# Transposes of a head moved to the score banks, with new step slots and a later rotation in layer 1

## What is computed

```python
def mixer_diff(h, w_in, lq1, lk1, lq2, lk2, sub_g, w_out, pos, ctx_k, ctx_v):
    z = h @ w_in                                   # 2048 x 8192
    q, k, v, g = jnp.split(z, idx, axis=-1)        # 16 heads, q and k 2 x 64, v 128
    qr = rope_2d(q, row, col)                      # latent tokens only
    k_all = jnp.concatenate([rope_2d(k, row, col), ctx_k], axis=1)
    v_all = jnp.concatenate([v, ctx_v], axis=1)
    s = jnp.einsum('bqhmd,bshmd->bhmqs', qb, k).astype(F32) * scale
    p = jax.nn.softmax(s, axis=-1)
    w = (p[:, :, 0] - lam * p[:, :, 1]).astype(v.dtype)
    o = jnp.einsum('bhqs,bshe->bqhe', w, v)
    o = rms_norm(o, sub_g) * (1 - LAMBDA_INIT_1)
    out = (o.reshape(b_, t, C_V_WIDTH) * jax.nn.silu(g)) @ w_out
```

## Time and profile before

| | |
|---|---|
| runs | 2828.07, 2830.34, 2833.81 us |
| median | 2830.34 us |
| profiled execution, device time | 2835.45 us |
| its span, first to last instruction | 2833.9 us |
| mean granted TensorE clock | 0.963 of full speed |
| TensorE matmul busy | 2570.7 us, 91% |
| VectorE, ScalarE, GpSimd busy | 1722.7, 810.6, 426.5 us |
| HBM traffic | 140 GB/s over the span |

### The profile page before, as it was taken

How to read it: one execution, slowest core, us unless ns; L and a number is a source line. 1 busy time by engine, 2 the same in 40 slices (tenths; PEclk the granted TensorE clock), 3 DMA queues, 4 the chain that set the end, 5 groups by cost and what they waited for, 6 DMA issues and landing times.

```text
span 2833.9 us, 38154 instructions
## 1 busy us (share of the span) xinstructions
PE 2570.7 (91%) x12040; PEld 2020.2 (71%) x12040; DVE 1722.7 (61%) x3165; ACT 810.6 (29%) x1698; POOL 426.5 (15%) x481
## 2 busy tenths in 40 slices
PE   6999999998888889979999999998999999978995
PEld 1258877777776768867877777777777777856884
DVE  1335777877777546766456555665666565554676
ACT  2112222222222222223233333333333333322221
POOL 0000222211222010000121212222221211011001
PEclk8999999999999989989999999999999999988998
DMA  7745544444443455554422222322232322245555
GB/s 268 251 141 174 184 138 147 128 146 150 161 161 116 144 211 182 193 189 138 136 93 86 90 72 85 95 91 85 73 97 84 97 86 93 84 135 205 182 193 200
DMA packets 165601, 395.42 MB, mean 140 GB/s; under 512 B 15008, under 2 KB 15648, under 8 KB 160992
## 3 DMA queue, kind: packets, MB, share of 16 engines
q1 hardware_dynamic: 132304, 249.08, 27.9%
q0 software_dynamic: 33168, 144.72, 14.5%
HBM read 332.93 MB, written 63.18 MB: 140 GB/s over the span
## 4 chain that ended last, share of the span: by engine, by line
PE 64%; DVE 17%; DVEq 7%; issue 5%; ACT 3%; DMA 3%; POOL 0%; ACTq 0%; SPq 0%; POOLq 0%
PE ps L554 49%; DVE w_lo L1128 4%; PE ps L440 3%; PE ps L449 3%; PE ps L583 3%; PE ps L458 3%; DVE small L1005 2%; DVE work L1022 2%; DVEq L1151 2%; DMA w_raw<-in_w_ada_dram 1%; ACT w_hi L773 1%; PE ps L541 1%; DMA stage<-z 1%; DMA o<-work 1%; DVEq L1237 1%
## 5 line engine op out<-in xcount | busy, mean ns | idle before, releaser
L554 PE MATMUL ps<-w_hi,hT_hi 128*128 128x512 f32 x2800 | 1149.6, 411 | 14.3 <-issue 7.6
L554 PE MATMUL ps<-w_hi,hT_lo 128*128 128x512 f32 x2800 | 1111.1, 397 | 0.0
L554 PE MATMUL ps<-w_lo,hT_hi 128*128 128x512 f32 x2800 | 1106.6, 395 | 0.0
L1128 DVE TENSOR_TENSOR w_lo<-w_raw,w_hi 128x512 fp32r<-128x512 f32 x560 | 408.0, 729 | 372.4 <-ACT w_hi L773 354.1
L554 PEld LDWEIGHTS ps<-w_hi,hT_lo 128*128 128x128 f32 x2800 | 534.1, 191 | 120.0
L554 PEld LDWEIGHTS ps<-w_hi,hT_hi 128*128 128x128 f32 x2800 | 536.1, 191 | 110.6 <-issue 12.3
L554 PEld LDWEIGHTS ps<-w_lo,hT_hi 128*128 128x128 f32 x2800 | 536.4, 192 | 92.6 <-issue 1.4
L773 ACT CAST w_hi<-w_raw 128x512 fp32r<-128x512 f32 x560 | 346.9, 621 | 486.3 <-PE ps L554 467.8
L1158 DVE SCALAR_TENSOR_TENSOR ada_sum<-w_raw,cond,ada_sum 128x512 f32<-128x512 f32 x480 | 365.8, 803 | 35.4 <-issue 10.3
L724 ACT ACTIVATE work<-ps,small 128x640 f32<-128x640 f32 (+1 forms) x200 | 142.1, 710 | 574.4 <-DVE small L1008 574.3
L440 PE MATMUL ps<-consts,work 128*128 128x128 f32 x768 | 133.7, 288 | 74.5 <-DVE q_low_lo L997 19.7
(11 more groups left out here) (185 smaller groups left out, 2426.9 us busy)
## 6 DMA issues: line engine op xcount, KB each, us to landing
w_raw<-in_w_in_dram SPq DMA_DIRECT2D x216, 512.0 KB, 4.0
w_raw<-in_w_ada_dram SPq DMA_DIRECT2D x256, 256.0 KB, 3.0
z<-stage POOLq DMA_DIRECT2D x27, 1280.0 KB, 5.1
w_raw<-in_w_ada_dram SPq DMA_DIRECT2D x64, 512.0 KB, 4.7
w_raw<-in_w_out_dram SPq DMA_DIRECT2D x64, 512.0 KB, 4.1
work<-z POOLq DMA_DIRECT2D x72, 320.0 KB, 3.7
work<-o POOLq DMA_DIRECT2D x8, 1280.0 KB, 8.1
x<-stage POOLq DMA_DIRECT2D x7, 1280.0 KB, 11.7
```

What stands on the lines that cost most here:

```text
L554: last = nc.tensor.matmul(ps[:, t, :], x[:, kt, t * P:(t + 1) * P], w[:, kt % RING, :], start=(kt == 0 and i == 0), stop=(kt == KT - 1 and ...
L1128: nc.vector.tensor_tensor(w_lo[:, kt % RING, :], w_raw[:, w_at(c, kt), kt % 2, :], w_hi[:, kt % RING, :].bitcast(F32), ALU.subtract).then_ ...
```

## The change

1. turn_bank: T1 (k) goes to bank 6 and T2 (mixed) to bank 7, the score banks; every other T stays in bank 5. T1 and T2 no longer wait for bank 5 but for the last exponential of the head before. In both layers. In layer 0 the wait for mod_free stands at T2 in place of S0. S0 still waits until T0, T1 and T2 have been read (t_free, four counts).
2. ORDER1: S9 stands ahead of T6 (it was behind it), so S8 and S9 follow each other.
3. AT1: new slots. T1 2 to 1, T2 4 to 2, S1 10 to 11, S2 14 to 15, S3 18 to 19, T3 24 to 26, S4 26 to 27, S7 40 to 39, S8 44 to 43, S9 48 to 45, T6 45 to 47, P1 52 to 53, B1 54 to 55; the others stand. S2 goes from row 2 to row 3, T3 from row 4 to row 5, S7 from row 8 to row 7.
4. head1: GpSimd loads q, k and v of the next head, stores the head before, then waits for P0 of the current head (pv_ready) and only then rotates.

```diff
-ORDER1 = ["T", "T", "T", "S", "S", "S", "S", "T", "S", "T", "S", "T", "S", "P", "S", "B", "S", "T", "S",
+ORDER1 = ["T", "T", "T", "S", "S", "S", "S", "T", "S", "T", "S", "T", "S", "P", "S", "B", "S", "S", "T",
           "T", "T", "P", "B", "T", "P", "B"]
...
-AT1 = [0, 2, 4, 7, 10, 14, 18, 24, 26, 28, 31, 32, 35, 36, 40, 41, 44, 45, 48, 49, 51, 52, 54, 56, 58, 59]
+AT1 = [0, 1, 2, 7, 11, 15, 19, 26, 27, 28, 31, 32, 35, 36, 39, 41, 43, 45, 47, 49, 51, 53, 55, 56, 58, 59]
...
+        def turn_bank(r):
+
+            return {1: SC, 2: SC + 1}.get(r, TURN)
...
-                bank_free(q)
+                bank = turn_bank(q)
+                if bank == TURN:
+                    bank_free(q)
+                else:
+                    pe.wait_ge(s.s_exp, h * NS + 1)
+                if bank == MOD_ROWS[0] and L.n == 0:
+                    pe.wait_ge(mod_free, 9 if isinstance(h, int) and h == 7 else h + 3)
                 for n, src in enumerate(blocks):
-                    last = nc.tensor.transpose(ps[:, TURN, n * P:(n + 1) * P], src, ident)
+                    last = nc.tensor.transpose(ps[:, bank, n * P:(n + 1) * P], src, ident)
...
                         pe.wait_ge(s.t_free, h * NF + 4)
-                        if L.n == 0:
-                            pe.wait_ge(mod_free, 9 if isinstance(h, int) and h == 7 else h + 3)
...
-                    last = nc.scalar.copy(dst[r0:r1, :], ps[r0:r1, TURN, c0:c1])
+                    last = nc.scalar.copy(dst[r0:r1, :], ps[r0:r1, turn_bank(r), c0:c1])
...
                 next_qk(L1, h + 1)
-                rotate_head(L1, h + 1)
                 if v:
                     next_v(L1, h + 1)
                 if not first:
                     store_head(L1, h - 1)
                     free_head(L1, h - 1)
+                wait(S[1].pv_ready, h * 3 + 1)
+                rotate_head(L1, h + 1)
```

More of the change, by code:

```diff
@@ L996, in turn @@
                     r0, r1 = rows or (0, P)
-                    last_op = nc.vector.tensor_tensor(lo[r0:r1, :], ps[r0:r1, TURN, c0:c1],
+                    last_op = nc.vector.tensor_tensor(lo[r0:r1, :], ps[r0:r1, turn_bank(r), c0:c1],
                                                       hi[r0:r1, :].bitcast(F32), ALU.subtract)
```

## The result

The kernel after takes 2845.08 us, the median of five runs from 2841.71 to 2852.37 us, against 2830.34 us before, which is the median of five runs too. The ratio is 1.0052, with a 95% interval of 1.0036 to 1.0067: slower by 0.5%. The forecast was 2842 us. The profiled execution has a span of 2846.6 us (before 2833.9) and a mean granted clock of 0.955 (before 0.963).

The account below looks back on a forecast made before the run. TensorE, busy 91%, bounds the kernel; time is lost where it waits. Layer 0 -12, first twelve heads -33 +46 +18 -9 +10, last four -8: together +12 us, 2842 us against the median 2830.34; range 2808 to 2866.

Parts of the forecast that it names:

- The opening: Layer 1 heads, T0 to T3: waits fall from 5.3 to 2.6 us a head, -33 us over the first twelve.
- the heavier rival: Layer 1: opening gives only 1.5 us a head, collision takes 2.4 us; +33 us, 2863 us; chance 0.15.
- S9: First twelve layer 1 heads: S9 stalls 3.8 us (2.0 to 4.4) for S8's exponential, +46 us.
- The price of the collision: Rotation after P0 in layer 1 lengthens VectorE's split 10 and combine(3): +1.8 us within the S9 stall.
- The clock: Behind the S9 stall TensorE falls to half clock: +1.5 us a head (0 to 1.6), +18 us over twelve.
- The rival in which the clock stays up: Behind S9: collision without a fall of the clock, -6 us, 2824 us; chance 0.17.
- the point of decision: At S9: below a stall of some 2.5 us the missed collision, with the clock staying up, would hold.
- Other waits of the second half: First twelve heads: S8, T6, P1 waits gone, -9 us; new S6 and T9 waits of 0.4 us each, +10.
- Layer 0: Seven heads of layer 0: T1's waits and three half-clock stretches saved, -12 us (-8 to -15).
- The last four heads and the rest: Last four layer 1 heads: opening -11, S9 stall +8, T9 less T6 and P1 -2, clock -3; -8 us.
- The sum: Whole kernel: all terms together +12 us on the profiled 2835.45 us; 2842 us against the median; chance 0.50.
- The rival on the other side: Layer 1: rotation and combine(3) miss each other, S9 stalls 2.0 us; -28 us, 2803 us; chance 0.15 (-28 to -15).

Follow-up runs that it names:

- kernel 2: Kernel before with only the new banks for T1 and T2; old order, slots and rotation: 2793.07 us, ratio 0.9872.
- kernel 5: Kernel before with only GpSimd's rotation moved behind P0 of the current head; old banks, order and slots: 2814.4 us, ratio 0.993.
- kernel 1: Kernel after with GpSimd's rotation back directly behind the loads of q and k; new banks, order and slots: 2828.06 us, ratio 0.9998.
- kernel 3: Kernel after with the second half of a head back in its old order and slots (S7, S8, T6, S9): 2780.41 us, ratio 0.9825.
- kernel 6: Kernel 3 with S7 at slot 39 (row 7) in place of 40, T6 still between S8 and S9: 2805.65 us, ratio 0.9897.
- kernel 4: Kernel after with S7 alone back at slot 40 (row 8) in place of 39: 2808.01 us, ratio 0.9931.
- Kernels 7 and 8: First: kernel 3 with the rotation behind combine(3), 2770.51 us, ratio 0.9777. Second: the first with T3, S4, T4 one slot later, 2769.16 us, ratio 0.9768.

## Why the prediction was right

**The opening.** Forecast 5.3 to 2.6 us of waits a head, measured 5.30 to 2.51. S0 0.67 (0.9), S3 0.69 (0.7), T3 1.03 (1.0), while T1 and T2 follow T0 at one slot's distance without a wait. The chains laid out from the earlier trace rows held, and the heavier rival, in which S0 and S3 inherit T1's wait, is out: S0 took over 0.44 us of it and S3 nothing (kernel 2). The gain was put down to the banks and the new slots together, though, and what the new opening slots give by themselves no kernel shows. An estimate from kernels 2 and 5 says little or nothing: kernel 5, with the old slots and the rotation late, loses 3.63 us from T0 to T3; less its waits at T1 and T2 (1.42 and 0.18) and plus the 0.44 that S0 inherits, that would be 2.5 us, as measured with the new slots (2.51).

**S9.** Forecast 3.8 us, measured 4.01. S7's exponential starts 2.16 us behind S7, the split ends at 5.09 (forecast 4.3 plus its part of the collision), combine(3) at 8.46 (6.5 plus 1.8), S9 starts at 9.62 (9.4). Two links of the chain were a little short: the split starts 1.72 us behind the exponential (forecast 1.43), and S9 starts 1.16 us behind the combine's end. The sum has 1.1 for the latter, read as the end of S8's exponential; the earlier trace rows give 1.02 to that end. The price of the collision, +1.8, was taken out of 0 to 2.4 (a stall of 2.0 to 4.4); kernel 1 has it at 1.64. The trace agrees with the rule that the prediction took from the Trainium skill, page "SBUF — State Buffer", section "Who interferes with whom", by which the operation that starts first keeps the port: GpSimd's L1518 started at 1606.06, the combine at 1606.18 and took 1.82 us, while L1518 took its usual 1.26. By kernels 3 and 6 the combine loses 0.40 to 0.97 us beside the same rotation, as the phase has it.

**The clock: the term that was mis-sized.** I took 3.3 us at half clock, 1.5 us a head, from the stretches behind the stalls of layer 0. The mechanism was right, but the stretch behind S9 is 5.9 us long in the head shown and 5.1 us on average of the twelve, and everything besides the waits grew by 1.95 us a head. That is 23 us for 18 forecast. The rival in which the clock stays up is out for a stall of 4 us. At 2.3 us (kernel 1) the fall comes in six of twelve heads, at 3.0 us (kernel 6) in seven of twelve, and at 1.8 to 1.9 us in heads 12 to 14 of kernel 4 in all three. So the point of decision which I gave, a stall of some 2.5 us, set between the 2.0 us that left the clock up and the 3.4 us that did not, is no point: the length of the stall alone does not decide it.

**Other waits of the second half.** -0.75 and +0.8 us a head forecast; S6 has 0.43 (0.4), T9 0.45 (0.4), T6 stays at 0.20 and T8 at 0.18. Measured +0.29 a head where I had +0.08: 2.5 us.

**Layer 0.** Forecast -12, measured -15.3. The eight kernels with the same layer 0 (the kernel after and all but kernel 5) reach the first T0 of layer 1 after 1417.5 to 1424.3 us, 15 to 22 us earlier than the kernel before, so this forecast was low by 3 to 10 us. The steps of the eight heads themselves last 640.9 us before and 625.6 after, and in the other seven kernels 620.8 to 624.1. TensorE was at 0.50 for 58.0 us of them before and for 44.4 after, which fits the stretches that were to go, but does not explain the spread: the fastest of the eight, kernel 4, has 47.8 us at 0.50 and kernel 6 has 37.5. Of the 6.8 us of spread, 3.5 lie ahead of the first projection (166.0 to 169.5 us). What makes the rest of the gain and of the spread stays open.

**The last four heads and the rest.** Forecast -8, measured -13.7. Waits up to T3 fall from 3.87 to 0.26 us a head (forecast to 1.0), -14 us for -11, and S9 waits 1.27 us, +5 for +8.

**The sum.** The errors are -3 and -6 on one side, +5 (clock), +2 (S9) and +3 (others) on the other: +12.7 on the span for +12 forecast. The nearness of the total is partly luck; each term lay within 6 us. The rival on the other side, a collision that misses, would by these numbers have saved 1.64 us of stall and 1.15 of clock a head: an estimate of 2845 - 12 x 2.8 = 2811 us, where the prediction had 2803.

**What the forecast could not see.** It called the second half the part that decides and was right, but summed it up as one stall. The square of experiment 6 shows two edits with a price of their own, either of which can be taken back alone. The banks give 37 us, the new opening and late rotation together another 13 on top of them (kernel 3), and the right place for the rotation 10 to 14 more (medians, ratios). Kernels 7 and 8, at 2770.5 and 2769.2 us, are 2.2 to 2.3% faster than the kernel before.

## What to carry to other kernels

When a step is moved by one slot, look first at whether it crosses a border of the other engines' queues: here one slot of S7 put a split of the weights into a chain and cost 25 to 37 us by the medians, where a slot is 0.68 us. Price a collision where it falls: the same GpSimd work cost 1.6 us a head on a chain without cover, 0.9 at most on one with cover, and 0.26 us a head once it began behind the operation that mattered. And add to a stall of TensorE of about 2 us or more the stretch of half clock that may follow it; test it in the stage in question, since its length differs from that in another stage.

## What the runs showed of the hardware that I had not expected

- Half clock behind a stall lasts differently long. Behind 3.4 us in layer 0 it was about three microseconds; behind 4.0 us at S9 the windows show 0.50 from 1609.1 to 1615.0 us, and behind the same stall in heads 0, 1, 4 and 8 it was 3.4 us.
- The same stall is followed by half clock in one head and not in another of one execution: 2.30 us with 1.00 behind it and 2.29 us with 0.71 over 5.8 us in kernel 1. A stall of 3.0 us in kernel 6 left the clock up in five of twelve heads, and one of 1.8 to 1.9 us in kernel 4 was followed by 0.50 in all of heads 12 to 14. What decides between them I did not find.
- A small shift of GpSimd's work against VectorE's changes the price of a collision: in the kernel before, combine(0) took 0.89 us where it started 3.34 us behind the start of the rotation (the head of the earlier trace rows), and 1.82 us where it started 3.58 us behind it (head 10). Over all kernels the combine's last operation took 0.88, 1.28, 1.82 or 2.0 us and a split 0.69 to 1.83, beside the same eight operations.
